# Identity products on TensorE in the waiting places of the expert routing and of the combination after layer 0

## The reference

```python
h = modulate(rmsnorm(x, norm_ffn_g[l]), sh2, sc2)
x = x + g2[:, None, :] * grouped_moe(h, router_w, router_bias,
                                     expert_w_gate[l], expert_w_up[l], expert_w_down[l])
...
scores = jax.nn.sigmoid((hf @ router_w).astype(jnp.float32))
_, top_idx = lax.top_k(jnp.where(in_group, biased, -jnp.inf), TOP_K)
...
return (jax.nn.silu(xb @ w_gate[e]) * (xb @ w_up[e])) @ w_down[e]
```

## Time and profile before

| | us |
|---|---|
| three runs | 1473.43, 1475.39, 1479.84 |
| median | 1475.39 |
| profiled execution, device time | 1473.27 |
| profiled execution, span of the records | 1471.5 |
| TensorE busy in it | 1272.6 (86%) |
| VectorE, ScalarE, GpSimd busy | 924.1, 584.3, 167.0 |

### The profile page before, as it was taken

The page is one execution under the profiler, slowest core; times in us unless marked ns, Lnnn a source line. Parts: engine busy times, 40 slices in busy tenths (PEclk is TensorE's granted clock), DMA queues, the critical chain, the costliest instruction groups (busy, mean ns, idle before and its releaser), DMA issues.

```text
span 1471.5 us, 14017 instructions
## 1 busy us (share of the span) xinstructions
PE 1272.6 (86%) x4745; PEld 799.2 (54%) x4745; DVE 924.1 (63%) x1308; ACT 584.3 (40%) x782; POOL 167.0 (11%) x181
## 2 busy tenths in 40 slices
PE   1699989937999999985799999999289999999881
PEld 1444434525777766642688854445266667777430
DVE  5468984456777777722866587725677777777114
ACT  2236300325555555511512156612355555555001
POOL 4000001010000000002000047700110000000002
PEclk9799999958999999998899999999589999999996
DMA  9934668134999999893476440031359999998454
GB/s 357 374 116 143 209 194 354 43 133 175 355 365 366 365 377 376 306 363 106 154 268 201 143 172 1 1 129 39 141 204 370 386 366 366 366 365 314 165 185 185
DMA packets 79614, 353.11 MB, mean 240 GB/s; under 512 B 12696, under 2 KB 12880, under 8 KB 70608
## 3 DMA queue, kind: packets, MB, share of 16 engines
q1 hardware_dynamic: 64576, 326.65, 60.0%
q0 software_dynamic: 8352, 20.46, 3.8%
q10 hardware_dynamic: 6640, 5.42, 1.1%
HBM read 334.15 MB, written 28.31 MB: 246 GB/s over the span
## 4 chain that ended last, share of the span: by engine, by line
PE 77%; DVE 12%; ACT 3%; DMA 3%; issue 2%; ACTq 1%; POOL 1%; DVEq 0%; POOLq 0%; SPq 0%
PE ps L1631 24%; PE ps L1642 16%; PE ps L1730 8%; PE ps L1572 8%; PE ps L1544 6%; PE ps L1622 3%; DVE scratch L914 3%; PE ps L1617 2%; PE ps L1774 2%; PE ps L1802 2%; PE ps L1788 2%; PE ps L1636 1%; ACTq L659 1%; PE ps L1505 1%; DMA gate_rows<-in_lru_wx_dram 1%
## 5 line engine op out<-in xcount | busy, mean ns | idle before, releaser
L1642 PE MATMUL ps<-slab_ring,scratch 128*128 128x512 f32 x560 | 246.5, 593 | 3.4 <-ACT scratch L835 2.1
L1631 PE MATMUL ps<-slab_ring_r,gate_rows_r 128*128 128x512 f32 x512 | 201.9, 394 | 0.0
L1642 PEld LDWEIGHTS ps<-slab_ring,scratch 128*128 128x128 f32 x560 | 105.8, 190 | 124.2 <-issue 117.3
L1303 DVE TENSOR_TENSOR slab_ring_r<-slab_ring,h_t_r 128x2048 fp32r<-128x2048 f32 x64 | 143.8, 2288 | 21.9 <-ACT h_t_r L787 21.8
L1544 PE MATMUL ps<-h_t,slab_ring 128*128 128x512 f32 x320 | 142.0, 603 | 12.4 <-DMA gate_rows<-in_lru_wx_dram 12.4
L1730 PE MATMUL ps<-slab_ring_r 128*128 128x512 f32 x384 | 121.0, 396 | 3.0 <-DVE h_t_r L971 3.0
L1631 PE MATMUL ps<-h_t_r,gate_rows_r 128*128 128x512 f32 x256 | 106.0, 414 | 14.7 <-DVE scratch_r L1297 11.1
L787 ACT ACTIVATE h_t_r<-slab_ring 128x2048 fp32r<-128x2048 f32 x64 | 118.4, 1901 | 0.2 <-issue 0.2
L1544 PEld LDWEIGHTS ps<-h_t,slab_ring 128*128 128x128 f32 x320 | 62.0, 194 | 91.3 <-issue 78.5
L1631 PEld LDWEIGHTS ps<-slab_ring_r,gate_rows_r 128*128 128x128 f32 x512 | 98.1, 192 | 19.2 <-issue 0.5
L1631 PE MATMUL ps<-h_t_r,scratch_r 128*128 128x512 f32 x256 | 102.1, 399 | 0.0
(11 more groups left out here) (296 smaller groups left out, 2039.0 us busy)
## 6 DMA issues: line engine op xcount, KB each, us to landing
slab_ring<-in_expert_w_gate_dram SPq DMA_DIRECT2D x35, 2048.0 KB, 10.1
slab_ring<-in_expert_w_up_dram SPq DMA_DIRECT2D x35, 2048.0 KB, 10.2
slab_ring<-in_expert_w_down_dram SPq DMA_DIRECT2D x35, 2048.0 KB, 10.1
mod_ring<-in_mod_w_dram SPq DMA_DIRECT2D x48, 512.0 KB, 4.6
y_rows<-scratch SPq DMA_DIRECT2D x35, 512.0 KB, 10.7
slab_ring<-in_mod_w_dram SPq DMA_DIRECT2D x32, 512.0 KB, 5.0
slab_ring<-in_w_qkv_dram SPq DMA_DIRECT2D x6, 2048.0 KB, 11.7
slab_ring<-in_w_in_ab_dram SPq DMA_DIRECT2D x5, 2048.0 KB, 23.0
```

The lines of the kernel that those rows point to most:

```text
L1303: tt_(rest, w, top.bitcast(F32), ALU.subtract).then_inc(low_ready[c], 1)
L1631: ins = pe.matmul(ps[:, bank, :], x, w, start=(kt == 0 and i == 0), stop=(kt == KT - 1 and i == 2))
L1642: ins = pe.matmul(ps[:, 5 + h, :], hidT[:, f, :], w[:, 2 * f + h, :], start=(f == 0), stop=(f == FT - 1))
```

## The change

`experts` gets a helper that issues a number of identity products into the first 128 columns of PSUM bank 3, and six calls of it. Ahead of the wait for the last tile's normed rows stand 36 products, ahead of its router products 30, ahead of the ranks 34, ahead of the slot sums 44, behind them (and so ahead of the gathered rows) 46, and behind the first gathered rows' transposes 26. The function runs for both layers. Between layer 0's experts and `turn_x(2, 0)` TensorE now waits for `comb_filled[0]` and then issues 50 products into bank 7. None of the products signals a semaphore.

```diff
+            def keep_clock(products):
+
+                for _ in range(products):
+                    pe.matmul(ps[:, 3, 0:P], ident[:, :], ident[:, :], start=True, stop=True)
+
...
                 if t:
                     logits(t - 1)
+            keep_clock(36)
             turn_x(s, TT - 1)
+            keep_clock(30)
             logits(TT - 1)
 
+            keep_clock(34)
             pe.wait_ge(hot_ready, TT * (l + 1))
...
             ins.then_inc(rank_ready, 1)
 
+            keep_clock(44)
             pe.wait_ge(place_ready, l + 1)
...
             ins.then_inc(slots_summed, 1)
+            keep_clock(46)
...
             turn_xs(0, xs_turned)
+            keep_clock(26)
             step(0, 0, 0, first=1)
...
         experts(0)
 
+        pe.wait_ge(comb_filled[0], 32)
+        for _ in range(50):
+            pe.matmul(ps[:, 7, 0:P], ident[:, :], ident[:, :], start=True, stop=True)
         turn_x(2, 0)
```

## The result

The changed kernel takes 1506.1 us (median of four runs, 1506.0 to 1506.4) against 1475.6 for the kernel before (a fourth run has joined the three of the table above). The ratio is 1.020 with a 95% interval of 1.018 to 1.023, so it is slower by 30.5 us. The profiled execution took 1505.96 us with a span of 1504.2, 32.7 more than the profiled execution of before.

What follows compares the result with a forecast made beforehand. TensorE, busy 86% of the span, was taken as the bound, with a serial chain in the routing. Two layers at 10.5 us (16.7 less 6.2) plus 3.4 at the combination gave 24.4, so 1499.8 us, range 1491 to 1514.

Steps and rivals of the forecast that it cites:

- The sign, the place and the mechanism: Whole kernel: slower (chance 0.87), through routing batches outlasting their waits in both layers and a late combination.
- A product is two records: Added identity products on TensorE: each float32 product makes two records, so 964 added records, against 482 at one each.
- A product costs 0.215 us: Added 128-column products at the high clock: 0.215 us each, a quarter of a 512-column down product's 0.859.
- the first rival: Routing batches: products at 0.1075 us fit inside their waits, so the kernel gets faster, 1463.0 us; chance 0.09.
- Each batch costs what it outlasts its wait by: Six routing batches: 46.4 us against 28.7 of idle time, less 1.0, add 16.7 us per layer, net 10.5.
- One serial chain: Routing: each of six waits ends with work begun only after TensorE's previous step, so any delay delays all behind it.
- What the clock gives back, 6.2 us a layer: Routing steps at the high clock: transposes 1.86, router products 1.72, slot sums 0.94, step 0's start 1.68 us.
- The combination adds 3.4 us: After layer 0: the batch of 50 ends at 709.1, making VectorE's step and the products behind it 3.4 us later.
- Step 1's wait moves along: Expert step 1: its 3.71 us wait for VectorE shifts with step 0's delay, slow start included, and absorbs nothing.
- The cheap product as rival: Routing batches: at 0.1075 us a product nothing is late and 6.2 us per layer return, 1463.0 us; chance 0.09.

Runs made afterwards that it cites:

- e1: The changed kernel with every batch at half its number (18, 15, 17, 22, 23, 13 per layer, 25 at the combination): 1467.3 us, ratio 0.994 to the kernel before.
- e3: The changed kernel with full-number routing batches of identity transposes in place of products, nothing at the combination: 1467.6 us, ratio 0.995 to the kernel before.
- e6: Against e1, the batch ahead of the first gathered rows back at 46 products from 23: 1479.3 us, ratio 1.003 to the kernel before.
- e2: The kernel before with only the wait and the 50 products after layer 0, none in the routing: 1478.8 us, ratio 1.004.
- e5: Against e1, batches fitted to its waits (20, 20, 19, 24, 26, 15), 16 more ahead of step 1's wait, none at the combination: 1460.6 us, ratio 0.990.
- e4: Against e1, each product with 16 columns in place of 128, nothing at the combination: 1502.2 us, ratio 1.019 to the kernel before.
- e9: Against e5, wide products among the last tile's router products, 21 ahead of them, and batches in the crowded experts' blocks' waits: 1456.7 us, ratio 0.989.

## Why the prediction was right

The sign, the place and the mechanism held, and 1506.1 lies between 1491 and 1514. The forecast of 24.4 us against 30.5 measured was low by a fifth, and each term can be checked.

- *A product is two records.* Right: 964 were added. This and not the clock decided the case. e1 and e3 show it from both sides: half the products, or as many instructions of one record each, turn the loss into a gain.
- *A product costs 0.215 us.* Too low. It is 0.225 (48.6 / 216). I let the time go by columns alone, from a neighbour of 512 of them. A record of 512 columns costs 0.430 us and one of 128 costs 0.1125, and a straight line through the two leaves some 7 ns a record beside the columns. That is an estimate from two points; no run tested another width above 16. The miss is 2.2 us per layer and the largest. The Trainium skill, "FP8 and Floating Point Precision", "TensorE Precision Notes", gives four passes to a true float32 product, and "TensorE: Matmul & The Clock Gate", "Back-to-back issue gap", gives 128 / 2.4 + 2.5, some 56 ns, to one isolated pass. Four of these are 0.223 us, an estimate from the two pages, and the trace agrees with 0.225, though it shows two records and no passes. The 81 ns that the Trainium skill gives for sustained streams in the same section, behind the first rival, is not what a float32 product cost here.
- *Each batch costs what it outlasts its wait by.* Right, shown by e6 in one place (3.8 us against 4.1), and by the missing brackets in the rows above. Layers 0 and 1 got 12.6 and 12.8 us longer; 10.5 + 2.2 is 12.7. The first gate products came 15.2 us later than 337.06, 0.9 of it from before the routing, where I had named some 12; that is the product's price again.
- *One serial chain.* Not quite. The second wait did not end with work that began when TensorE's step before was done: VectorE's choice for tile 2 set its end (e1). It cost the forecast nothing, because with full batches TensorE itself is the path.
- *What the clock gives back, 6.2 us a layer.* Right in the changed kernel: 1.04, 1.04 and 1.86 us for the transposes and router products, 1.04 for the slot sums (0.84 gained where I took 0.94), and the first nine spacings of step 0 in 2.17 us (352.27 to 354.44) against 2.16. But it is not all to be had by a kernel whose batches fit: there VectorE holds back the last router products, as e1 showed, and the first 0.9 us is gone.
- *The combination adds 3.4 us.* Right in kind, too low by 0.7. In the changed kernel 17.7 us lie between the landing and the first product of L1730 (710.21 to 727.89, there L1744) against 13.6, 4.1 more, and 4.2 in e2; that its medians differ by 3.4 is luck. I had VectorE's step at the end of the transposes, 3.4 us late. It was 3.7 late, since the batch took 13.0 us and not 12.7, and VectorE's wait of 0.44 us for ScalarE had no term.
- *Step 1's wait moves along.* Right: 3.72 us, as before. That it stayed is what e5 gained on.
- *The cheap product as rival.* It did not come about, but e1, e3 and e5 are that case made true by other means. It brought 8 us in e1 and e3, where I had 12.4, and 15 in e5, which also fills step 1's wait. I had put the price that decides at 0.133 us, where a batch just fills its wait. The sign turns higher, at about 0.16, since the 1.0 and 6.2 us that come back per layer, less the combination's share, pay for some overshoot as well: (28.7 + 1.0 + 6.2 - 1.7) / 216. The 0.225 measured lies above both.

Between the two profiled executions lie 32.7 us, 8.3 more than the 24.4 of the forecast. They are 4.4 for the product's price, 0.7 at the combination, 0.3 in the rest of the stretch between the layers, 1.7 for a block of L1622 that met the lower clock, 0.9 in a stretch that the change doesn't touch, and 0.3 unplaced.

## What to carry to other kernels

Work put into a wait to keep the clock up must end before the wait does, since TensorE's stream runs in order and the filler is then the thing waited for. Price it by records at the clock that it will run at, from a batch that was measured, not from the count in the source: a float32 product is two records, a float32 transpose is one. And look at the granted clock rather than at the busy row: in e4 products of 16 columns filled every wait of the routing, and the clock was 0.50.

## What the runs showed of the hardware that was not expected

- With products of 16 columns in the waits the granted clock was 0.50 from 324 to 332 us, with TensorE busy for 8.00 of 8.00 us (e4). With the same numbers of products of 128 columns (e1), and with transposes of 128 columns (e3), it was 1.00 there. Behind the last router products it fell in one layer and not in the other with 0.4 us idle ahead of them (e5), and in both with 1.5 us (e1). What share the idle time and what share the narrow products have in that, no run separates.
- The same kind of block of 32 records (L1622 and its later line numbers) took 14.0 us in one execution and 15.7 in another, with the same wait ahead of it, and another block of the changed kernel 16.55 (1418.59). Filling these waits made all three 14.0 (e9). Such places are a likely source of the spread of some 6 us between runs of one kernel; that the spread would vanish with them was not shown.
- The clock can fall while the engine works. In e4 it fell inside a batch with no idle time ahead. In the changed kernel step 1 started at the higher level behind 3.72 us of waiting (spacing 0.31 us, 368.08 to 368.39), and some products later the spacing was 0.43 us (369.11 to 369.54), that of the lower one. If the wait is what brought that fall, which was not tested, its cost is paid after the restart, at a place that shows no wait.
